# Joining two stages of a fused block: the mixer runs into the latent attention without a barrier, and three column sums move into the attention

## The chip, the cores and the metric

One core of a Trainium2 chip runs the whole program. The metric is the device time of one execution in microseconds, the median over several executions. The chip's engines are TensorE (PE in the profile, with its weight loads as PEld), VectorE (DVE), ScalarE (ACT), GpSimd (POOL) and SyncE (SP, which issues the DMAs). Each works through its own list in order and waits for others on semaphores.

## The reference, cut to what matters

Two transformer-like blocks of two layers each run over 512 tokens of width 1024. The change is in the second block, in each of its two layers. Such a layer splits its projection in four branches:

```
y_a = conformer_conv(...)   # 31-tap convolution, then layer_norm over 256 features, then silu
y_b = hgrn2_bidir(...)      # gated scan; o = rms_norm per head of 64 features, times silu(g)
y_c = short_gated_conv(...)
y_d = mla(...)              # q, k normed over 96 features per head, rope, softmax(q k^T / sqrt(96)) v
cat = rms_norm_2(concatenate([y_a, y_b, y_c, y_d]))   # in four groups of 256 features
x = x + cat @ w_out ; then attention over mem (256 rows), then a feed-forward part
```

Three of the norms matter here: the root mean square of `y_b` per head (two slots of 128 features, so two sums), and the variance of `y_a` after its mean is taken off (one sum over 256 features).

## The kernel before, in words

Everything lies transposed: features on the 128 partitions, the 512 tokens along the free axis. A tile of 128 x 512 float32 is called a slot (`S[:, n, :]`). PSUM has eight banks of 128 x 512. A norm is made of three steps: ScalarE squares the slots, TensorE multiplies a constant matrix (`ones` for a sum over all features, `heads` for sums over 64) with the squares, and ScalarE turns the sum into a factor by a logarithm and an exponential with scale -0.5. Both functions and the square stand in one table set.

The second block's layer is three stages, each a `nc.Block()` in which every engine gets its list: `second_mixer`, `second_attention` (called latent attention here) and `second_tail`. A stage closes with `sem.stage_end()` (line 334 on): all engines meet in a barrier, and the stage's semaphores, a contiguous range of numbers, are cleared by one instruction (line 337), so that the next stage can count them from zero.

**The end of the mixer.** After the scan, PE makes the projections of queries, keys and values, the mean of branch A (L1917), a rotation (L1921), `key_sum(0..3)` (L1904, the sum over 96 features for each head's key) and between them the query sums (L1931, 24 small products of 4 columns). Then come the products in question: two with `heads` for branch B into banks 5 and 6 (L1940) and two that add up the variance of branch A in bank 7 (L1943). ACT makes `key_root(h)` (a logarithm L2052 and an exponential L2054) for each head, in between the squares of branch B (L2066) and of the centred branch A (L2073), the copies of the values out of PSUM (L2069) and the query factor (L2076, L2078); it ends with three logarithms (L2083 twice, L2085). DVE makes `key(0)` (L2245), four `query_rope` (L2250), then `key(1..3)` (L2245), each of which needs its head's factor. POOL makes the rope part of the keys (L2311).

**The latent attention** has 16 units: four heads by four blocks of 128 queries. Unit n passes: PE scores (L743, a float32 product, which shows as two instructions of 128x512) into bank n mod 4; DVE maximum (L841) and its negative (L844); ACT exponential with its sum (L805); DVE reciprocal of the sum (L854), one step later; POOL scaling (L880) into a ring of four; PE transposes (L751) into bank 4 or 5, four units later; ACT copy to `PT` (L814); after eight units the product with the values (L757) into bank 6, and ACT's copy out (L823). PE goes in steps of two units, the others in steps of one. Bank 7 is used by nobody. Functions `side_act`, `side_dve`, `side_pool` and `side_pe` put other work behind each step. Before the change these are: a preamble of three exponentials on ACT (L2337), which finish the factors of which the mixer left the logarithms; from step 2 on ACT the squares of the memory input (L529), from step 3 on DVE its scaling (L523), its low part (L533) and the adding of squares (L540), eight of each; branch A times its factor on DVE in steps 3 and 4 (L2361), branch B in steps 5 and 6 (L2365); branch B times its gate on POOL at units 8 and 10 (L2380); weight tiles split in high and low parts on ACT (L367, steps 10, 12, 14) and POOL (L376, units 12 and 14). The input `mem` is loaded by SP at the stage's start (L2333). At its end ACT makes branch A's silu and the squares for the tail, and a barrier follows.

The order on each engine is written out by hand; nothing is planned at run time. A wait holds everything behind it on its engine.

Of the kernel before, what the change touches and what calls it, by code (L numbers as in the profile page):

```python
# [18 lines left out]
ALU = mybir.AluOpType  # L19
# [297 lines left out]
class Semaphores:  # L317


    def __init__(self, nc):  # L320
        self.nc, self.stream, self.stage, self.numbers = nc, {}, {}, []
        for name in ["tile_done", "tile_high", "tile_low"] + [f"tile_in_{i}" for i in range(RING)]:
            self.stream[name] = nc.alloc_semaphore(name)

    def __call__(self, name):
        if name in self.stream:
            return self.stream[name]
        if name not in self.stage:
            if len(self.stage) == len(self.numbers):
                self.numbers.append(self.nc.alloc_semaphore(f"stage_{len(self.numbers)}"))  # L330
            self.stage[name] = self.numbers[len(self.stage)]
        return self.stage[name]

    def stage_end(self):
        numbers = sorted(s.num for s in self.numbers)
        assert numbers == list(range(numbers[0], numbers[-1] + 1))
        self.nc.all_engine_barrier(sems_to_clear=range(numbers[0], numbers[-1] + 1))  # L337
        self.stage = {}

# [252 lines left out]
def build(nc, x_in, w1, small1, const_in, p_in, w2, small2, masks_in, mem_in, pos_in, out):  # L592
# [108 lines left out]

    def attention_work(*kinds, side_act=None, side_dve=None, side_pool=None, side_pe=None):

# [15 lines left out]
        def width(n):  # L719

            return units[n][0]["width"](units[n][3])
# [14 lines left out]
        def run_pe(pe):  # L736
            def scores(n):
                a, h, g, i = units[n]
                for m in range(a["maps"]):
                    s = first[n] + m  # L740
                    if s >= 4:
                        pe.wait_ge(sem("max_ready" if biased else "exp_done"), s - 3)
                    pe.matmul(banks[s % 4][:, 0:width(n)], a["q"](h, m, i), a["k"](h, m, width(n)), start=True,  # L743
                              stop=True).then_inc(sem("scored"), 1)

            def turn(n):
                pe.wait_ge(sem("prob_ready"), n + 1)
                if n >= 2:
                    pe.wait_ge(sem("pt_ready"), n - 1)
                for j in range(width(n) // P):  # L750
                    mm = pe.transpose(banks[4 + n % 2][:, j * P:j * P + P], prob(n)[:, j * P:j * P + P], cst("ident"))  # L751
                mm.then_inc(sem("transposed"), 1)
# [132 lines left out]

    def attention(weights, prefetch, work, before=None, first_act=None):

        run_pe, run_act, run_dve, run_pool = work
        with nc.Block() as block:
            @block.sync  # L890
            def _(sp):
                if before:
                    before(sp)
                weights.load(sp, prefetch)

            @block.tensor
            def _(pe):
                run_pe(pe)
# [8 lines left out]
            def _(dve):  # L907
                run_dve(dve)

            @block.gpsimd  # L910
            def _(pool):
                run_pool(pool)
        sem.stage_end()

# [786 lines left out]
    QUERY_R, EPS96 = 36, 54  # L1701
    B_R, DEVIATION, KEY_R = 36, 44, (45, 46, 47, 38)
    NL = len(LEVELS)
    PAD = 15

    def second_mixer(layer, weights, prep):

        base = DEPTH * FIRST_TILES + layer * SECOND_TILES
        latent_at = base + N_PROJ2
# [61 lines left out]
        with nc.Block() as block:  # L1771
# [6 lines left out]
            def _(pe):  # L1778
# [158 lines left out]
                pe.sem_inc(sem("tile_done"), 2)  # L1937
                for c in range(2):
                    pe.wait_ge(sem("b_square"), c + 1)
                    pe.matmul(banks[5 + c][:, :], cst("heads"), PT[:, 0, c, :], start=True, stop=True).then_inc(sem("b_sum"), 1)  # L1940
                for c in range(2):
                    pe.wait_ge(sem("centered_square"), c + 1)
                    mm = pe.matmul(banks[7][:, :], cst("ones"), PT[:, 0, 2 + c, :], start=(c == 0), stop=(c == 1))  # L1943
                mm.then_inc(sem("var_summed"), 1)

            @block.scalar
            def _(act):
# [115 lines left out]
                key_root(0)  # L2063
                for c in range(2):
                    act.wait_ge(sem("both"), c + 1)
                    act.activation(PT[:, 0, c, :], S[:, Y + 2 + c, :], ACT.Square).then_inc(sem("b_square"), 1)  # L2066
# [4 lines left out]
                for c in range(2):  # L2071
                    act.wait_ge(sem("centered"), c + 1)
                    act.activation(PT[:, 0, 2 + c, :], S[:, TAP_A + c, :], ACT.Square).then_inc(sem("centered_square"), 1)  # L2073
                act.wait_ge(sem("query_sum"), 1)
# [186 lines left out]
            def _(pool):  # L2261
# [50 lines left out]
        sem.stage_end()  # L2312

# [14 lines left out]
    def second_attention(layer, weights, memory):  # L2328

        base = weights.used  # L2330

        def before(sp):
            sp.dma_start(S[:, MEM_RAW:MEM_RAW + 4, :].rearrange("p a (b n) -> p (a b) n", b=2), mem_in).then_inc(sem("load_mem"), 16)  # L2333

        def first_act(act):
            for slot in (DEVIATION, B_R, B_R + 1):
                act.activation(S[:, slot, :], S[:, slot, :], ACT.Exp, scale=-0.5).then_inc(sem("late_rstd"), 1)  # L2337

        def side_act(act, step):
            if step == 2:  # L2340
                act.wait_ge(sem("load_mem"), 16)
            if 2 <= step < 2 + KC:
# [12 lines left out]

        def side_dve(dve, step, place):
            if place == "end" and step in (3, 4):
                a = S[:, TAP_A + step - 3, :]
                if step == 3:
                    dve.wait_ge(sem("late_rstd"), 3)  # L2360
                dve.tensor_tensor(a, a, S[:, DEVIATION, :], ALU.mult).then_inc(sem("standard"), 1)  # L2361
            if place == "end" and step in (5, 6):
                c = step - 5
                y = S[:, Y + 2 + c, :]
                dve.scalar_tensor_tensor(y, y, s2("onorm", c), S[:, B_R + c, :], ALU.mult, ALU.mult).then_inc(sem("b_normed"), 1)  # L2365
            if place == "scores" and step == 3:
# [8 lines left out]
        def side_pool(pool, n):  # L2375
            if n in (8, 10):
                c = (n - 8) // 2
                y = S[:, Y + 2 + c, :]
                pool.wait_ge(sem("b_normed"), c + 1)
                pool.tensor_tensor(y, y, S[:, G + c, :], ALU.mult).then_inc(sem("branch_b"), 1)  # L2380
            if n in (12, 14):
                weights.split_low(pool, base + n // 2 - 5)

# [4 lines left out]
            query_col=lambda h, i: col[:, QUERY_R + 4 * i + h:QUERY_R + 4 * i + h + 1]),  # L2388
            side_act=side_act, side_dve=side_dve, side_pool=side_pool), before, first_act)

# [387 lines left out]
```

## Time and profile before

| what | value |
|---|---|
| median of 3 runs | 3219.67 us (3214.8 to 3219.79) |
| the profiled execution | 3216.99 us, of which the span is 3215.2 us |
| mean granted TensorE clock | 0.984 of full speed |
| PE busy | 3066.1 us, 95% |
| latent attention, first layer | scores from 1903.24 us, next stage from 1953.36 us |
| latent attention, second layer | scores from 2674.20 us, next stage from 2724.61 us |

PE's share of 95% is a mean over stages with different limits: in the large dense products it is never idle, in the two latent attentions it waits often. A row of the timeline gives the start, how long the merged instructions took from the first start to the last end, the engine, the line, the operation, output <- input, the shape and the count; in square brackets the engine's idle time before it and what ended that. The granted clock is in parts of 2.4 GHz: 1.00 is 2.4 GHz and 0.5 is 1.2 GHz.

### The profile page before, as it was taken

Reading aid. Unit: us, or ns where it says so; the run is one execution under the profiler, and the core shown is the slowest. Engines: PE = TensorE matmul, PEld = TensorE weight load, DVE = VectorE, ACT = ScalarE, POOL = GpSimd, SP = SyncE. Lnnn points to the kernel's source line nnn. Section 1 sums busy time; section 2 is a strip of 40 time slices with the busy share of each in tenths; the row PEclk is TensorE's granted clock in tenths of the full one; section 3 lists DMA queues with packets and bytes.
Section 4 is the critical chain, followed back from the end, with each engine's and each line's share of the span. In section 5 each row is a group of like instructions: output and inputs, shape, how many; then the busy total and the mean of one; then the engine's idle time right before and its main releaser. Section 6 shows DMA issues by size and latency. Waiting matters only on the chain. (4 is left out here: it accounts for less than half of the span.)

```text
span 3215.2 us, 38320 instructions
## 1 busy us (share of the span) xinstructions
PE 3066.1 (95%) x14320; PEld 2394.0 (74%) x14320; DVE 1623.4 (50%) x2468; ACT 1327.0 (41%) x2194; POOL 1581.0 (49%) x862
## 2 busy tenths in 40 slices
PE   8989999999998999999999988899999988989999
PEld 6766788888766678888887756688888764768887
DVE  3863357732467434775348764433324955543321
ACT  4445433333443554333343475532323257442221
POOL 5634655554764455555565443344444534344443
PEclk9999999999999999999999989999999998999999
DMA  4211233333221123333323102233333211223333
GB/s 135 67 59 47 79 101 96 98 106 105 92 69 60 52 67 99 98 99 108 105 87 97 48 20 66 60 98 99 98 104 100 67 34 33 72 73 98 99 99 105
DMA packets 73736, 265.07 MB, mean 82 GB/s; under 512 B 8656, under 2 KB 9168, under 8 KB 73168
## 3 DMA queue, kind: packets, MB, share of 16 engines
q1 hardware_dynamic: 73552, 262.62, 26.6%
q8 instruction: 115, 1.88, 0.2%
q14 instruction: 69, 0.57, 0.1%
HBM read 260.49 MB, written 2.10 MB: 82 GB/s over the span
## 5 line engine op out<-in xcount | busy, mean ns | idle before, releaser
L376 POOL TENSOR_TENSOR low<-raw,high 128x1024 fp32r<-128x1024 f32 x482 | 1179.7, 2449 | 1148.8 <-ACT high L367 1115.5
L391 PE MATMUL bank<-slot_r,low 128*128 128x512 f32 (+1 forms) x3648 | 1423.8, 390 | 0.0
L392 PE MATMUL bank<-slot_r,high 128*128 128x512 f32 (+1 forms) x3648 | 1423.4, 390 | 0.0
L390 PE MATMUL bank<-slot_r,high 128*128 128x512 f32 (+1 forms) x3328 | 1323.8, 398 | 44.2 <-POOL low L376 15.0
L367 ACT ACTIVATE high<-raw 128x1024 fp32r<-128x1024 f32 x482 | 507.5, 1055 | 900.4 <-PE bank L392 826.7
L392 PEld LDWEIGHTS bank<-slot_r,high 128*128 128x128 f32 x3648 | 688.6, 189 | 147.2
L391 PEld LDWEIGHTS bank<-slot_r,low 128*128 128x128 f32 x3648 | 689.7, 189 | 144.5 <-issue 5.8
L390 PEld LDWEIGHTS bank<-slot_r,high 128*128 128x128 f32 x3328 | 629.0, 189 | 214.8 <-issue 50.3
L1624 DVE SCALAR_TENSOR_TENSOR tmp<-padded,small,tmp 128x512 f32<-128x512 f32 x176 | 209.7, 1249 | 0.0
L880 POOL TENSOR_SCALAR tmp<-tmp,stat 128x512 f32<-128x512 f32 (+3 forms) x128 | 79.9, 625 | 144.9 <-DVE stat L854 119.7
L2111 DVE SCALAR_TENSOR_TENSOR slots<-padded,small,slots 128x512 f32<-128x512 f32 x128 | 132.9, 1096 | 0.0
L1615 DVE TENSOR_TENSOR padded<-bank,rs 128x512 f32<-128x512 f32 x88 | 60.3, 686 | 138.9 <-PE bank L392 129.2
L2707 DVE TENSOR_TENSOR tmp<-bank,rs 128x512 f32<-128x512 f32 x44 | 30.4, 692 | 192.0 <-PE bank L392 186.8
L533 DVE SCALAR_TENSOR_TENSOR slot_r<-slots,small,slot_r 128x512 fp32r<-128x512 f32 (+1 forms) x80 | 93.5, 1168 | 44.0 <-ACT slot_r L520 43.7
L814 ACT ACTIVATE PT<-bank 128x256 f32<-128x256 f32 (+3 forms) x160 | 71.6, 453 | 104.8 <-PE bank L757 60.3
L743 PE MATMUL bank<-slots 64*128 64x256 f32 (+4 forms) x384 | 94.6, 501 | 18.2 <-PEq L337 15.4
L2619 ACT ACTIVATE tmp<-tmp 128x512 f32<-128x512 f32 x44 | 27.8, 632 | 203.0 <-DVE tmp L2707 203.0
L2717 DVE TENSOR_TENSOR tmp<-bank,rs 128x512 f32<-128x512 f32 x16 | 11.1, 691 | 193.1 <-PE bank L392 193.1
L751 PE MATMUL bank<-const,tmp 128*128 128x128 f32 x432 | 73.8, 294 | 36.3 <-ACT PT L814 27.6
L1367 DVE TENSOR_TENSOR slot_r<-tmp,slot_r 128x512 fp32r<-128x512 f32 x48 | 75.7, 1576 | 59.2 <-ACT slot_r L2612 59.2
L751 PEld LDWEIGHTS bank<-const,tmp 128*128 128x128 f32 x432 | 52.7, 148 | 68.2 <-issue 39.3
L390 PE MATMUL bank<-pt_r,high 128*128 128x512 f32 x256 | 101.1, 395 | 0.0
(316 smaller groups left out, 3134.4 us busy)
## 6 DMA issues: line engine op xcount, KB each, us to landing
raw<-w SPq DMA_DIRECT2D x482, 512.0 KB, 3.5
slots<-x_in SPq DMA_DIRECT2D x4, 512.0 KB, 6.5
slots<-mem_in SPq DMA_DIRECT2D x2, 1024.0 KB, 4.7
out<-slots SPq DMA_DIRECT2D x8, 256.0 KB, 4.6
const<-const_in SPq DMA_DIRECT2D x1, 1095.5 KB, 10.2
padded<-p_in SPq DMA_DIRECT2D x2, 512.0 KB, 5.1
tmp<-masks_in SPq DMA_DIRECT2D x1, 512.0 KB, 11.0
small<-small SPq DMA_DIRECT2D x2, 231.5 KB, 2.9
```

The source lines that it names most:

```text
L367: act.activation(self.high[:, t % PARTS, :], self.raw[:, t % RING, :], ACT.Copy).then_inc(self.sem("tile_high"), 1)
L376: pool.tensor_tensor(self.low[:, t % PARTS, :], self.raw[:, t % RING, :], self.high[:, t % PARTS, :].bitcast(F32), ALU.subtract).then_inc( ...
L390: pe.matmul(acc, lhs[0], rhs[1], start=first, stop=False)
L391: pe.matmul(acc, lhs[1], rhs[0], start=False, stop=False)
L392: return pe.matmul(acc, lhs[0], rhs[0], start=False, stop=last)
L533: dve.scalar_tensor_tensor(self.pairs[c][1], self.xs[c], self.gain[c], self.pairs[c][0].bitcast(F32), ALU.mult, ALU.subtract).then_inc(sel ...
L743: pe.matmul(banks[s % 4][:, 0:width(n)], a["q"](h, m, i), a["k"](h, m, width(n)), start=True, stop=True).then_inc(sem("scored"), 1)
L751: mm = pe.transpose(banks[4 + n % 2][:, j * P:j * P + P], prob(n)[:, j * P:j * P + P], cst("ident"))
L880: pool.tensor_scalar(prob(n), tmp[:, E + s % 4, 0:width(n)], st(3, s), 1.0, ALU.mult, ALU.mult).then_inc(sem("prob_ready"), 1)
L1367: dve.tensor_tensor(parts[g][1], tmp[:, 6 + g % 2, :], parts[g][0].bitcast(F32), ALU.subtract).then_inc(sem("hidden_low"), 1)
L1624: dve.scalar_tensor_tensor(o, padded_t[:, s % 4, 15 - tap:15 - tap + SEQ], s1("conv_w", (2 - tap) * 2 * FC + ch), o, ALU.mult, ALU.add).th ...
L2111: ins = dve.scalar_tensor_tensor(o, src, s2(w, 2 * j + c), o, ALU.mult, ALU.add)
```

## The change

The barrier between `second_mixer` and `second_attention` is gone. Semaphores are now named by a part ("mixer" or "latent") and a name, so both stages can count in one stretch, and the attention names the mixer's semaphores for which it must wait. The barrier behind the attention stays. The two `heads` products and the variance product leave the mixer's PE list and go into the attention's steps 2, 4 and 6 ("turns"), all through bank 7, one after the other; their logarithm and exponential become ACT's side work of steps 3, 5 and 7; the squares go to the end of ACT's mixer list, into slots of their own. Branch B's scaling on DVE moves to steps 6 and 7, branch A's to 8 and 9; POOL's gate products move to units 10 and 12, its weight splits to 11 and 13. ACT's preamble of three exponentials is dropped.

```diff
@@ class Semaphores
+    def of(self, part, name):
+        key = (part, name)
+        if key not in self.stage:
+            if len(self.stage) == len(self.numbers):
+                self.numbers.append(self.nc.alloc_semaphore(f"stage_{len(self.numbers)}"))
+            self.stage[key] = self.numbers[len(self.stage)]
+        return self.stage[key]
@@ second_mixer, tensor
-                for c in range(2):
-                    pe.wait_ge(sem("b_square"), c + 1)
-                    pe.matmul(banks[5 + c][:, :], cst("heads"), PT[:, 0, c, :], start=True, stop=True).then_inc(sem("b_sum"), 1)
-                for c in range(2):
-                    pe.wait_ge(sem("centered_square"), c + 1)
-                    mm = pe.matmul(banks[7][:, :], cst("ones"), PT[:, 0, 2 + c, :], start=(c == 0), stop=(c == 1))
-                mm.then_inc(sem("var_summed"), 1)
@@ second_mixer, scalar (squares and logarithms leave their old places)
-                    act.wait_ge(sem("b_sum"), c + 1)
-                    act.activation(S[:, B_R + c, :], banks[5 + c][:, :], ACT.Ln, scale=1.0 / 64, bias=eps).then_inc(sem("b_root"), 1)
-                act.wait_ge(sem("var_summed"), 1)
-                act.activation(S[:, DEVIATION, :], banks[7][:, :], ACT.Ln, scale=1.0 / 256, bias=eps).then_inc(sem("deviation"), 1)
+                    act.activation(S[:, B_SQ + c, :], S[:, Y + 2 + c, :], ACT.Square).then_inc(sem("b_square"), 1)
+                act.wait_ge(sem("centered"), 2)
+                for c in range(2):
+                    act.activation(S[:, A_SQ + c, :], S[:, TAP_A + c, :], ACT.Square).then_inc(sem("a_square"), 1)
@@ end of second_mixer
-        sem.stage_end()
@@ second_attention
         def before(sp):
+            sp.wait_ge(mixer("v_evac"), 2)
+        def scores_ready(pe, n):
+            if n == 0:
+                pe.wait_ge(mixer("query_done"), 4)
+                pe.wait_ge(mixer("key_done"), 2)
+                pe.wait_ge(mixer("key_rope"), 2)
+                pe.wait_ge(mixer("key_log"), 3)
+            if n == 1:
+                pe.wait_ge(mixer("query_log"), 1)
+            if n == 3:
+                pe.wait_ge(mixer("key_done"), 4)
+                pe.wait_ge(mixer("key_rope"), 4)
+        def side_pe(pe, step, place):
+            if place == "turns" and step in (2, 4):
+                c = step // 2 - 1
+                if c == 0:
+                    pe.wait_ge(mixer("centered"), 2)
+                else:
+                    pe.wait_ge(sem("b_log"), 1)
+                pe.wait_ge(mixer("b_square"), c + 1)
+                pe.matmul(banks[7][:, :], cst("heads"), S[:, B_SQ + c, :], start=True, stop=True).then_inc(sem("b_sum"), 1)
+            if place == "turns" and step == 6:
+                pe.wait_ge(sem("b_log"), 2)
+                pe.wait_ge(mixer("a_square"), 2)
+                for c in range(2):
+                    mm = pe.matmul(banks[7][:, :], cst("ones"), S[:, A_SQ + c, :], start=(c == 0), stop=(c == 1))
+                mm.then_inc(sem("var_summed"), 1)
         def first_act(act):
-            for slot in (DEVIATION, B_R, B_R + 1):
-                act.activation(S[:, slot, :], S[:, slot, :], ACT.Exp, scale=-0.5).then_inc(sem("late_rstd"), 1)
+            act.wait_ge(mixer("query_rstd"), 1)
+            act.wait_ge(mixer("cos_done"), 1)
         def side_act(act, step):
+            if step in (3, 5):
+                c = (step - 3) // 2
+                r = S[:, B_R + c, :]
+                act.wait_ge(sem("b_sum"), c + 1)
+                act.activation(r, banks[7][:, :], ACT.Ln, scale=1.0 / 64, bias=eps).then_inc(sem("b_log"), 1)
+                act.wait_ge(sem("b_log"), c + 1)
+                act.activation(r, r, ACT.Exp, scale=-0.5).then_inc(sem("b_rstd"), 1)
+            if step == 7:    # the same for the variance: Ln, Exp into DEVIATION
...
         def side_dve(dve, step, place):
-            if place == "end" and step in (3, 4):      # branch A; branch B in (5, 6)
+            if place == "end" and step in (6, 7):      # branch B; branch A in (8, 9)
...
-            if n in (8, 10):
+            if n in (10, 12):
...
-            if n in (12, 14):
+            if n in (11, 13):
```

## Rows read from the trace of the kernel before

**Rows 1.** The page, engines' busy time over the whole span.

```profile
PE 3066.1 (95%) x14320; PEld 2394.0 (74%) x14320; DVE 1623.4 (50%) x2468; ACT 1327.0 (41%) x2194; POOL 1581.0 (49%) x862
```

**Rows 2.** Timeline of the first layer's joint: start, us, engine, line, operation, count.

```profile
1897.73 1.95 PE L1940 MATMUL bank<-PT,const 128*128 128x512 f32 x4
...
1899.53 1.88 PE L1943 MATMUL bank<-PT,const 128*128 128x512 f32 x4
...
1901.44 0.69 ACT L2085 ACTIVATE slots<-bank,const 128x512 f32<-128x512 f32 x1 [0.72 <-PE bank L1943]
...
1903.21 1.67 ACT L2337 ACTIVATE slots<-slots 128x512 f32<-128x512 f32 x3 [1.08 <-PEq L337]
1903.24 7.08 PE L743 MATMUL bank<-slots 96*128 96x512 f32 x12 [1.83 <-PEq L337]
```

**Rows 3.** Timeline of the second layer's joint.

```profile
2664.32 1.06 ACT L2069 ACTIVATE slots<-bank 128x512 f32<-128x512 f32 x2
...
2665.28 3.19 PE L1904 MATMUL bank<-tmp,const 96*128 96x512 f32 x4
...
2666.52 1.13 ACT L2073 ACTIVATE PT<-slots 128x512 f32<-128x512 f32 x2
...
2668.53 1.54 DVE L2245 SCALAR_TENSOR_TENSOR slots<-bank,small,slots 64x512 f32<-64x512 f32 x2
...
2669.91 0.63 ACT L2054 ACTIVATE slots<-slots 128x512 f32<-128x512 f32 x1
...
2670.57 0.76 DVE L2245 SCALAR_TENSOR_TENSOR slots<-bank,small,slots 64x512 f32<-64x512 f32 x1 [0.49 <-ACT slots L2054]
...
2674.20 5.39 PE L743 MATMUL bank<-slots 96*128 96x512 f32 x12 [1.83 <-PEq L337]
```

**Rows 4.** Timeline of the second layer's attention, units 0 to 12.

```profile
2676.31 0.78 ACT L805 ACTIVATE tmp<-bank,stat,col 128x512 f32<-128x512 f32 x1 [0.46 <-DVE stat L844]
...
2679.04 0.34 DVE L523 TENSOR_SCALAR slot_r<-slots,small 128x256 fp32r<-128x256 f32 x1
...
2680.36 0.68 DVE L841 TENSOR_REDUCE stat<-bank 128x1 f32<-128x512 f32 x1
...
2681.32 0.78 ACT L805 ACTIVATE tmp<-bank,stat,col 128x512 f32<-128x512 f32 x1 [0.83 <-DVE stat L844]
...
2682.57 0.41 ACT L529 ACTIVATE slots<-slots 128x256 f32<-128x256 f32 x1
...
2682.86 0.68 DVE L841 TENSOR_REDUCE stat<-bank 128x1 f32<-128x512 f32 x1
...
2687.99 0.69 DVE L841 TENSOR_REDUCE stat<-bank 128x1 f32<-128x512 f32 x1
...
2689.89 0.69 DVE L841 TENSOR_REDUCE stat<-bank 128x1 f32<-128x512 f32 x1
...
2694.30 1.26 POOL L2380 TENSOR_TENSOR slots<-slots 128x512 f32<-128x512 f32 x1
...
2694.54 1.17 DVE L523 TENSOR_SCALAR slot_r<-slots,small 128x256 fp32r<-128x256 f32 x1
...
2697.39 0.78 ACT L805 ACTIVATE tmp<-bank,stat,col 128x512 f32<-128x512 f32 x1 [0.43 <-DVE stat L844]
...
2699.45 5.35 PE L757 MATMUL bank<-PT,slots 128*64 128x512 f32 x16
```

**Rows 5.** Timeline of the first layer's attention, unit 11 and the first value product.

```profile
1927.86 0.78 ACT L805 ACTIVATE tmp<-bank,stat,col 128x512 f32<-128x512 f32 x1 [0.44 <-DVE stat L844]
...
1929.92 3.65 PE L757 MATMUL bank<-PT,slots 128*64 128x512 f32 x16
```

**Rows 6.** Windows at each attention's start: busy us by engine, granted clock after POOL's column.

```profile
1903.00:1911.00 8.00, 7.76 (x20) 3.75 (x21) 5.18 (x15) 5.75 (x13) 2.37 (x3) 0.79 0.38 131
...
2674.00:2682.00 8.00, 7.80 (x24) 3.78 (x24) 6.41 (x20) 6.31 (x14) 2.75 (x3) 1.00 0.38 131
```

**Rows 7.** Line L337, the barrier's instructions: ns min/median/max.

```profile
L337 POOLq EVENT_SEMAPHORE_RANGE_CLEAR  x13: 113/283/437, 26.4 to 3214.6; - x13
```

More of the change, by code:

```diff
@@ L320, in __init__ @@
     def __init__(self, nc):
-        self.nc, self.stream, self.stage, self.numbers = nc, {}, {}, []
+        self.nc, self.stream, self.stage, self.numbers, self.part = nc, {}, {}, [], ""
         for name in ["tile_done", "tile_high", "tile_low"] + [f"tile_in_{i}" for i in range(RING)]:
@@ L337, in stage_end @@
         self.nc.all_engine_barrier(sems_to_clear=range(numbers[0], numbers[-1] + 1))
-        self.stage = {}
+        self.stage, self.part = {}, ""
 class Weights:
@@ L884, in attention_work, with attention @@
         return run_pe, run_act, run_dve, run_pool
-    def attention(weights, prefetch, work, before=None, first_act=None):
+    def attention(weights, prefetch, work, before=None, first_act=None, first_dve=None, first_pool=None, joined=False):
         run_pe, run_act, run_dve, run_pool = work
@@ L911, in _ @@
             def _(pool):
+                if first_pool:
+                    first_pool(pool)
                 run_pool(pool)
-        sem.stage_end()
+        if not joined:
+            sem.stage_end()
     weights = Weights(sem, raw, high, low, [w1[l, t] for l in range(DEPTH) for t in range(FIRST_TILES)]
@@ L1706, in second_mixer @@
     def second_mixer(layer, weights, prep):
+        sem.next_part("mixer")
         base = DEPTH * FIRST_TILES + layer * SECOND_TILES
@@ L2063, in _ @@
                 key_root(0)
-                for c in range(2):
-                    act.wait_ge(sem("both"), c + 1)
-                    act.activation(PT[:, 0, c, :], S[:, Y + 2 + c, :], ACT.Square).then_inc(sem("b_square"), 1)
+                act.wait_ge(sem("both"), 2)
                 act.wait_ge(sem("v_projected"), 1)
@@ L2339, in side_act, with turn_ready @@
-        def side_act(act, step):
+        def scores_ready(pe, n):
[9 more added lines that the diff above has]
+                pe.wait_ge(mixer("key_rope"), 4)
+        def turn_ready(pe, n):
+            if n == 0:
+                pe.wait_ge(mixer("key_log"), 4)
@@ new lines, in first_act, with first_dve, first_pool @@
+        def first_act(act):
+            act.wait_ge(mixer("query_rstd"), 1)
+            act.wait_ge(mixer("cos_done"), 1)
+        def first_dve(dve):
+            dve.wait_ge(mixer("pv_done"), 8)
+        def first_pool(pool):
+            pool.wait_ge(mixer("query_done"), 4)
+            pool.wait_ge(mixer("key_sum"), 4)
+            pool.wait_ge(mixer("key_rope"), 4)
+        def side_act(act, step):
+            if step in (3, 5):
[6 more added lines that the diff above has]
+            if step == 7:
+                r = S[:, DEVIATION, :]
+                act.wait_ge(sem("var_summed"), 1)
+                act.activation(r, banks[7][:, :], ACT.Ln, scale=1.0 / 256, bias=eps).then_inc(sem("a_log"), 1)
+                act.wait_ge(sem("a_log"), 1)
+                act.activation(r, r, ACT.Exp, scale=-0.5).then_inc(sem("a_rstd"), 1)
@@ L2340, in side_act @@
             if step == 2:
                 act.wait_ge(sem("load_mem"), 16)
+                act.wait_ge(mixer("branch_c"), 2)
             if 2 <= step < 2 + KC:
@@ L2356, in side_dve @@
         def side_dve(dve, step, place):
-            if place == "end" and step in (3, 4):
-                a = S[:, TAP_A + step - 3, :]
-                if step == 3:
-                    dve.wait_ge(sem("late_rstd"), 3)
+            if place == "end" and step in (6, 7):
+                c = step - 6
+                y = S[:, Y + 2 + c, :]
+                dve.wait_ge(sem("b_rstd"), c + 1)
+                dve.wait_ge(mixer("b_square"), 2)
+                dve.scalar_tensor_tensor(y, y, s2("onorm", c), S[:, B_R + c, :], ALU.mult, ALU.mult).then_inc(sem("b_normed"), 1)
+            if place == "end" and step in (8, 9):
+                a = S[:, TAP_A + step - 8, :]
+                if step == 8:
+                    dve.wait_ge(sem("a_rstd"), 1)
+                    dve.wait_ge(mixer("a_square"), 2)
                 dve.tensor_tensor(a, a, S[:, DEVIATION, :], ALU.mult).then_inc(sem("standard"), 1)
[L2362 to L2365, printed above, removed]
             if place == "scores" and step == 3:
@@ L2388, in second_attention @@
             query_col=lambda h, i: col[:, QUERY_R + 4 * i + h:QUERY_R + 4 * i + h + 1]),
-            side_act=side_act, side_dve=side_dve, side_pool=side_pool), before, first_act)
+            side_act=side_act, side_dve=side_dve, side_pool=side_pool, side_pe=side_pe, scores_ready=scores_ready, turn_ready=turn_ready),
+            before, first_act, first_dve, first_pool, joined=False)
     def second_tail(layer, weights, memory, lead):
```

29 lines of the change are left out of this document (17 added, 12 removed).

## The prediction

> **What bounds the kernel now.** The page first: PE is busy 95% of 3215.2 us [rows 1], so at large the dense products set the time, and only stages in which PE waits can give anything. The two latent attentions are such stages, and both lie between barriers, so whatever comes earlier at the barrier behind them comes earlier at the end. The timeline of the joint shows what the change aims at: the sums of branch B and the variance hold PE from 1897.73 to 1901.41, ACT takes the last logarithm until 1902.13, the barrier lets go at 1903.2, PE has then been idle for 1.83 us, and ACT spends 1.67 us on three exponentials first [rows 2]. The second layer repeats it 771 us later: scores at 2674.20, first softmax exponential at 2676.31 [rows 3, 4]. Inside the attention the timeline of units 3 to 10 shows a DVE without idle time: a step lasts 2.50 us where it carries a piece of branch A or B (2680.36 to 2682.86) and 1.90 us where it does not (2687.99 to 2689.89) [rows 4]. From the value product on, PE and ACT set the pace, with hardly any side work left.
>
> **The start (per layer; clock times are those of the second layer).** PE's last product that stays in the mixer ends at 2665.28 + 3.19 = 2668.47 [rows 3]. Score 0 waits for key(1), the first of two instructions that start at 2668.53 and take 1.54 us, so about 2669.3 instead of 2674.20: PE is 4.9 us earlier. DVE is later than PE: key(3) follows at 2670.07 and takes 0.76, to 2670.8; the exponential can start 0.96 us after a maximum does (2680.36 to 2681.32, [rows 4]), so at 2671.8 as far as DVE is concerned. ACT is later still. The squares that stood between the key factors are gone from there (1.13 us each pair, [rows 3]), so the last key's logarithm can start when PE ends, at 2668.5; with its exponential (together 1.30 us, by the 0.69 and 0.63 of such a pair in [rows 2, 3], overlapping a little) it is through at 2669.8. Behind it stand the four squares, 2 x 1.13 = 2.26 us, to 2672.05. The first softmax exponential starts there instead of 2676.31: **gain 4.3 us**. The dropped preamble (1.67), the three logarithms, the barrier (1.08 on ACT) and the wait for the products are all inside that figure and are not counted again. The memory input's DMA now waits only for the value copies, which end at 2665.4 [rows 3] at the latest, far ahead of its first reader. The weight splits, two units earlier on POOL, issue their next load earlier; nothing waits for it before the barrier.
>
> **What is given back.** In steps 3, 5 and 7 ACT has a logarithm and an exponential more: 1.30 us. An ordinary ACT step (exponential, copy, square) is 1.66 us, from 2681.32 to the square's end at 2682.57 + 0.41 [rows 4]; with the pair it is 2.96. DVE asks for the memory square of that step in the next one, 1.1 us after its own step began (maximum 0.68, its negative and the scaling of 0.34 come first), and has 1.90 or 2.50 us per step. In step 3 there is no copy yet and the branch work has left DVE, so DVE is fast: I get the square at 2677.3 where DVE would take it at 2676.35, a stall of 1.0. In step 5 it is 2.96 against 1.90 with some slack in hand, 0.9; in step 7 0.2, since DVE's steps 6 and 7 now carry the branch work. **Loss 2.1 us.** DVE's own branch work (four pieces, about 0.67 us each by the difference of 2.57 and 1.90) moves from steps 3 to 6 to steps 6 to 9, all within DVE's busy stretch: nothing. PE's products through bank 7 (0.94 us per sum at full clock, 1.88 us for two in [rows 2]) lie in PE's idle time; each waits for the logarithm before it, and the scores behind are wanted over a microsecond later. If this cover goes, it costs what the second rival says.
>
> POOL's gate product at unit 8 ran beside DVE's step 10 and stretched the memory scaling there from 0.34 to 1.17 us [rows 4]. At units 10 and 12 the memory work is over: **gain 0.8**. The Trainium skill (GPSIMD Engine Reference, Specifications) says the two engines share their SBUF interfaces and contend when DVE uses two ports or two inputs. By that rule the weight split, moved to unit 11, would do no harm either, since DVE then reads maxima from PSUM; without the rule the sum would lose this 0.8.
>
> At step 10 ACT has its weight split of 1.06 us behind exponential and copy and is no longer waiting for DVE: about 0.4 of the lead is lost. So the exponential of unit 11, and with it the value product, come 4.3 - 2.1 + 0.8 - 0.4 = **2.6 us** earlier in the second layer. From there on the chain is ACT's and is unchanged.
>
> **The clock.** In the first layer the scores ran at a granted clock of 0.79 on the mean over 8 us, in the second at 1.00 [rows 6]; so unit 11 came 1927.86 - 1903.24 = 24.6 us after the first score there and 2697.39 - 2674.20 = 23.2 us here [rows 2 to 5], 1.4 us later. The value product was the other way round: 3.65 us at full clock in the first layer, 5.35 in the second [rows 5, 4]. In the new first layer: with full clock 2.6 + 1.4 = 4.0; at half clock each score takes 1.7 instead of 0.9 us and the new product stands between scores 3 and 4, so DVE waits for PE at unit 4, and I get 0.6. Half and half: 2.3. In the second layer: 2.6 at full clock, -0.8 at half; I take seven to three, 1.6. The value products may swap their clocks, 1.7 us each way per layer: zero in the mean, kept for the range.
>
> The Trainium skill (TensorE: Matmul & The Clock Gate, Part 1) says that an array that has been idle runs at half clock until it has been busy again. By that, taking out an idle 1.83 us speaks for the better case in both layers, 4.0 + 2.6 = 6.6. The trace does not decide it: the same 1.83 us was followed by half clock in one layer and not in the other.
>
> **The barrier's clear.** The joined stage has some 19 semaphores more than the mixer's 74. The clear took up to 437 ns [rows 7], about 6 ns for each; 0.1 us more in each of the four barriers that are left, 0.4 in all. Bounds: 0 if it hides, 0.5 if every one counts.
>
> **Sum:** 2.3 + 1.6 - 0.4 = 3.5 us, in [rows 1] terms 0.1% of the span. The profiled execution took 3216.99 us, 1.8 more than its span, and so would take 3213.5. The median shown is 2.7 higher than it, which gives 3216.2; since the other executions lie on both sides (3214.8, 3219.67, 3219.79), I put the median at 3215.5. A difference of less than 0.2%, 6.4 us, is about what a measurement of this kernel cannot tell from none.
>
> **The rivals.** *All of the joint comes through.* Full clock for scores and value products in both layers: 4.0 + 2.6, and 1.7 for the second layer's value product, is 8.3 less 0.4, so 7.9: 3219.67 - 7.9 = 3211.8. For it: the two layers before show each half of it. Against: every stretch of low PE activity in the trace is followed by half clock somewhere.
>
> *The sums are a serial chain.* Each of the three needs PE, ACT, and again PE before the next may use bank 7, and both engines wait in order, with scores, transposes and softmax exponentials queued behind. If nothing covers them, each costs its product (0.94 at full, 1.9 at half clock) and the pair (1.30): three make 6.7 to 9.6 us against a start gain of 4.3, so 2.4 to 5.3 lost per layer and 4.8 to 10.6 in all: 3224.5 to 3230.3, 3227 in the middle. It decides from the point at which a sum costs more than 4.3/3 = 1.4 us; I reckon 0.7 on the mean. Against it: ACT waited 0.83 us for DVE in unit 4 [rows 4]. For it: ACT's 2.96 us per step is above DVE's.
>
> *The clock falls where it stood.* 0.6 and -0.8, and 1.7 lost in the first layer's value product: 1.9 slower with the clear, 3221.6, which is no measurable change.
>
> *The start is not early.* If score 0 waits longer than I see (POOL's rope part of the keys, 1.26 us per head, is its other source), the gain shrinks to the barrier's 1.1 us per layer and is eaten by the chains: 3220 to 3222.
>
> **Chances.** My forecast 0.50, with its own range 3212 to 3219; all through 0.20; serial chain 0.12; clock 0.12; late start 0.06. The range 3210 to 3223 takes in all but the chain and the far edges. Faster by over 0.2% (below 3213.2) is most of the second case and a part of the first: 0.32. Slower by over 0.2% (above 3226.1) is the half of the chain and a little of the rest: 0.09. Within: 0.59.
>
> **What would show it.** Right: the first score about 5 us after the last key_sum's start, with no idle time of PE above 1 us before it; first exponential 4.3 us earlier relative to L1904; in steps 3 to 7 DVE waits for ACT's L529 by 2 us in sum and not for PE; the memory scaling stays at 0.34 us throughout; the value product 2.6 us earlier. Wrong: DVE idle before L841 for PE in step 4 or later; ACT idle before its new logarithms by over 0.5 us; the transposes late enough that ACT's copies wait for them before the first value product; or half clock in both stretches in both layers.

## The result and the profile after

The changed kernel takes 3223.3 us (median of 16 runs, 3220.42 to 3224.54) against 3215.64 us before (16 runs, 3210.57 to 3219.91): ratio 1.0023, 95% interval 1.0016 to 1.0029. It is 7.7 us slower where I had forecast 4 us faster. The forecast started from the 3219.67 us of three executions; over 16 the kernel before stands 4.0 us lower, so what is compared below is the change and not the absolute time. The profiled execution has a span of 3222.4 us. Its page, the engines' busy time, against [rows 1]:

```profile
PE 3067.1 (95%) x14320; PEld 2392.0 (74%) x14320; DVE 1625.2 (50%) x2468; ACT 1327.3 (41%) x2194; POOL 1582.8 (49%) x862
```

The busy times and counts are those of before within 2 us, so the loss is in waits and in slow products, not in work. The timeline of the first layer's joint, to be held against [rows 2], shows both:

```profile
1896.24 2.59 PE L1920 MATMUL bank<-tmp,const 96*128 96x512 f32 x4
...
1901.16 1.13 ACT L2089 ACTIVATE slots<-slots 128x512 f32<-128x512 f32 x2
...
1902.86 6.07 PE L750 MATMUL bank<-slots 96*128 96x512 f32 x8 [4.03 <-PEq L1787]
...
1906.07 0.78 ACT L814 ACTIVATE tmp<-bank,stat,col 128x512 f32<-128x512 f32 x1 [3.78 <-DVE stat L853]
```

PE's last key sum (L1920, L1904 before) ends at 1898.83, and then PE has nothing for 4.03 us, until something on its own queue at line L1787. That line is `with nc.Block() as block:` of the mixer. All that was taken out is the clearing barrier; the Block itself ends with a meeting of all engines. Its queue instructions in the first layer, with the ns that each took:

```profile
L1787 PEldq DRAIN  x1: 2673/2673/2673, 1896.2 to 1896.2; - x1
L1787 ACTq DRAIN  x1: 2729/2729/2729, 1899.6 to 1899.6; - x1
L1787 POOLq DRAIN  x1: 1554/1554/1554, 1900.3 to 1900.3; - x1
L1787 DVEq DRAIN  x1: 1525/1525/1525, 1900.3 to 1900.3; - x1
L1787 SPq EVENT_SEMAPHORE  x1: 17/17/17, 1902.5 to 1902.5; - x1
```

Each engine drains its list, ACT last (1899.6 + 2.73, the end of the four squares that the change had put there), and at 1902.5 all go on together. The kernel before has the same instructions at its line L1771, ahead of those of the clearing barrier (L337, [rows 7]); I had looked at the second and not at the first:

```profile
L1771 PEldq DRAIN  x2: 4713/4713/4713, 1896.7 to 2667.7; - x2
L1771 ACTq DRAIN  x2: 717/717/717, 1901.4 to 2672.4; - x2
```

The second thing is the rate of the scores. Eight instructions (four scores) take 6.07 us in the first layer and 6.91 in the second; before, twelve took 7.08 and 5.39 [rows 2, 3]. The windows of the first 8 us of each attention, to be held against [rows 6] (granted clock: seventh figure, behind POOL's):

```profile
1903.00:1911.00 8.00, 8.00 (x14) 3.42 (x15) 4.71 (x14) 3.66 (x10) 2.01 (x3) 0.71 0.36 131
2676.00:2684.00 8.00, 8.00 (x11) 3.39 (x12) 3.89 (x11) 3.01 (x8) 1.39 (x2) 0.59 0.38 132
```

0.71 and 0.59 instead of 0.79 and 1.00: half clock, 1.2 GHz, for about the first 4.8 and 6.5 us. Half clock did not begin in PE's idle time. In the second layer of the kernel before it is there during the last two key sums (first window), and it is back at full while the moved sums run (second window):

```profile
2665.30:2668.30 3.00, 3.00 (x7) 1.25 (x7) 2.91 (x4) 2.94 (x8) 1.26 (x1) 0.60 0.00 0
...
2669.30:2672.30 3.00, 3.00 (x8) 1.04 (x6) 1.50 (x2) 2.36 (x5) 2.50 (x2) 1.00 0.00 0
```

In the changed kernel the same key sums are slow too (first window), but behind them PE does nothing (second window, busy 0.00) and the clock stays at half until the scores:

```profile
2668.50:2671.90 3.40, 3.40 (x6) 0.96 (x5) 3.27 (x5) 2.01 (x5) 1.69 (x2) 0.55 0.00 0
2672.00:2675.90 3.90, 0.00 (x0) 0.00 (x0) 1.94 (x3) 3.38 (x6) 2.23 (x2) 0.50 0.00 0
```

So before the change the four products of the sums had stood in PE's 4 us, and by their end the clock was up again for the scores. The third thing is DVE's waits in the second layer's attention until the value product (us in total, times, longest):

```profile
DVE stat L850 <- PE bank L750: 6.1, 5, 4.0
DVE slots L545 <- ACT slots L534: 1.3, 2, 0.8
DVE stat L863 <- ACT tmp L814: 0.3, 1, 0.3
```

Before, in the same stretch of the second layer, it was one wait for the first score and nothing for the memory square:

```profile
DVE stat L841 <- PE bank L743: 4.0, 1, 4.0
DVE stat L854 <- ACT tmp L805: 0.2, 1, 0.2
```

For all kernels below I measure one stretch in the profiled execution, from the start of the product that sums the mean of branch A (L1917 before; up to there nothing was changed) to the first product of the tail. Before: 66.0 and 66.3 us in the two layers. Changed: 67.6 and 68.6, so 4.0 us more in the stretch, out of 7.2 us that the spans differ by. The first value product comes 42.9 and 44.8 us behind the same start, against 42.5 and 41.1 before: 0.4 and 3.7 us later, where the forecast had it 2.3 and 1.6 us earlier. Of the rest, 1.9 lies ahead of that product in the first layer (1889.35 against 1887.42) and most of the remainder in the last tail, where the code is the same; these parts I did not trace to a cause. A single execution is not the median: over the 13 kernels of this document the stretch of the first layer starts anywhere from 1882.6 to 1889.6 us, though the code ahead of it does the same work in all. Therefore the medians say what a kernel gains, and the traces where.

### The profile page after: what moved, and what is told of

Same layout as the page of the kernel before. It is cut to its first block and busy times, and to the rows that moved or that the text cites. A ratio compares the mean times of both kernels' runs of the same rounds, so it can differ in the third digit from the quotient of the medians.

```text
span 3222.4 us, 38332 instructions
## 1 busy us (share of the span) xinstructions
PE 3067.1 (95%) x14320; PEld 2392.0 (74%) x14320; DVE 1625.2 (50%) x2468; ACT 1327.3 (41%) x2194; POOL 1582.8 (49%) x862
## 6 DMA issues: line engine op xcount, KB each, us to landing
tmp<-masks_in SPq DMA_DIRECT2D x1, 512.0 KB, 10.9
```

## The experiments

Each has its time against the kernel before on the same chip (medians of that: 3215.46, 3215.31 and 3215.39 us in the three groups), and an interval for the ratio.

**How much is the meeting, and how much the move of the sums?** Four kernels fill a table of three by two: two meetings, the Block's only, or none; sums kept in the mixer or moved.

```diff
@@ one Block: both stages put their lists in one
+        with nc.Block() as block:
+            shared[0] = Shared(block)      # entering it again gives the same block
             second_mixer(layer, weights, lead)
+            sem.next_part("latent")
             memory = memory_prep()
             second_attention(layer, weights, memory)
+        shared[0] = None
+        sem.stage_end()
```

> The changed kernel with mixer and latent attention in one Block, so that no engine meets another between them. Theory M (the meeting at the Block's end stayed, and the sums left PE with nothing to do ahead of it): the first score starts about 4 us earlier relative to key_sum's last product, right behind key(1), and no DRAIN stands between; per layer 3 to 4.5 us less than the changed kernel, 3215 to 3218 us where that takes 3223.3. Theory S (the sums are a serial chain that costs by itself): the score starts early, but the first value product does not come more than 1 us earlier; 3221 to 3223.

> Only the clearing barrier between mixer and attention is taken out (names by part, waits on the mixer's semaphores); the three sums, their squares and logarithms, ACT's three exponentials and the steps of the side work stay where they were before the change. Theory M: the meeting at the Block's end stays, so only the second meeting goes: 0.9 us per layer, less 0.5 for the longer clears: 1 to 2 us faster than before (3215.6 becomes 3214). Theory S: the same; if the whole joint were worth its 4 us without the sums' move, 3208.

> As the one before, and both stages in one Block: no meeting at all, sums kept in the mixer. Theory M: PE goes from the variance product to score 0 with under 0.5 us between instead of 1.8, so 1.5 to 2.5 us per layer faster than before, 3211 to 3213. Theory S says the same here and that this is the best of the four; theory M says that the kernel with one Block and moved sums is about as fast.

> The sums moved as in the change, and the clearing barrier put back between the stages (both meetings as before the change). This prices the move alone. Theory M: 0.9 us per layer slower than the changed kernel and 0.5 us back from shorter clears: 3224 to 3226, about 9 us slower than before; PE idle about 5 us ahead of score 0, which then runs at half clock. Theory S: the same total, but with the loss in steps 3 to 9 of the attention and not in its first four scores.

| median us, ratio to before (95%), stretch by layer | sums kept | sums moved |
|---|---|---|
| both meetings | 3215.5 (before), 66.0 / 66.3 | 3222.6, 1.0019 (1.0010 to 1.0027), 68.2 / 67.7 |
| the Block's only | 3216.8, 1.0002 (0.9993 to 1.0011), 64.2 / 64.2 | 3223.3 (changed), 1.0023, 67.6 / 68.6 |
| none (one Block) | 3211.5, 0.9989 (0.9980 to 0.9997), 63.2 / 63.2 | 3215.3, 1.0000 (0.9991 to 1.0008), 64.9 / 65.2 |

Down the columns: taking out the clearing barrier by itself gives nothing that can be measured (1.3 us slower and 0.7 slower, within the intervals), though the stretch with sums kept is 2 us shorter per layer in the trace; only the Block's end gives something, 8 us with sums moved, and 5.3 with sums kept, where the two intervals just overlap. Across: the move costs 7.2, 6.5 and 3.9 us; the first two are clear of the intervals, the third is not, and rests on the stretches, which are 1.7 and 2.0 us longer. So it is the move that makes the change slower, and the missing join that keeps it from being paid. The first and the third expectation came in (3215.3 and 3211.5 us). The second stood at 3214 and measured 3216.8, which is not told apart from it. The fourth missed: I had expected two meetings to be slower than one by another 1 to 2 us.

With one Block and sums moved, the second layer's joint is what I had drawn in the prediction:

```profile
2659.45 3.54 PE L1932 MATMUL bank<-tmp,const 96*128 96x512 f32 x4
2663.48 6.87 PE L750 MATMUL bank<-slots 96*128 96x512 f32 x8 [0.50 <-DVE slots L2261]
...
2666.69 0.78 ACT L814 ACTIVATE tmp<-bank,stat,col 128x512 f32<-128x512 f32 x1 [0.24 <-DVE stat L853]
```

Score 0 waits for key(1) and nothing else, 10.9 us behind the mean's product instead of 15.8: 4.9 us earlier, as forecast. The first softmax exponential comes at 14.1 instead of 17.9, 3.8 us earlier (forecast 4.3), since the scores run at 1.7 us each. The first value product comes 41.3 behind it in the second layer, against 41.1 before: nothing of the lead is left. (In the first layer it is 40.2 against 42.5, so 2.3 us are left there.) DVE's waits in the second layer from there to the value product:

```profile
DVE stat L850 <- PE bank L750: 2.5, 5, 0.7
DVE slots L545 <- ACT slots L534: 1.3, 2, 0.8
```

**Is it the clock?** The changed kernel, with products that nobody reads in PE's idle time.

```diff
                 pe.sem_inc(sem("tile_done"), 2)
+                pe.wait_ge(sem("centered"), 2)
+                for _ in range(4):
+                    pe.matmul(banks[7][:, :], cst("ones")[0:96, :], tmp[0:96, K_SQ + 3, :], start=True, stop=True)
```

> The changed kernel with four idle products (the shape of key_sum, into bank 7, read by nobody) at the end of the mixer's PE list, where PE has 4.0 us without work until the Block's end. Nothing of the order behind them changes. Theory C (the moved sums had kept PE's clock up; without them the first scores run at half clock): the scores go at full clock, the first softmax exponential comes 1 us and the first value product 2 to 3 us earlier relative to the mean's product, 4 to 6 us in all: 3218 to 3220. Theory S (the loss of the move sits in the logarithm and exponential steps of the attention): no more than 1 us, 3222 to 3224.

Measured 3216.1 us, ratio 1.0002 (0.9993 to 1.0011) against 1.0023 for the changed kernel: 7 us for work that does nothing, 2 us more than the clock theory had asked for. In the second layer PE stands idle for 0.56 us instead of 4.03, and eight score instructions take 3.67 us instead of 6.91:

```profile
2672.21 3.77 PE L1956 MATMUL bank<-tmp,const 96*128 96x512 f32 x8
2676.54 3.67 PE L750 MATMUL bank<-slots 96*128 96x512 f32 x8 [0.56 <-PEq L1787]
```

```profile
1904.00:1912.00 8.00, 7.86 (x25) 4.00 (x26) 5.56 (x17) 5.26 (x13) 2.30 (x3) 1.00 0.38 131
2676.50:2684.50 8.00, 7.96 (x25) 4.11 (x26) 5.66 (x17) 5.37 (x13) 2.31 (x3) 1.00 0.38 132
```

Full clock in both. Score 0 is later than in the changed kernel (14.6 us behind the mean's product against 13.5 and 14.4), and the stretch is still 1.3 and 1.9 us shorter. The first exponential comes at 16.8 in both layers (16.7 and 17.6 in the changed kernel), the value product at 42.6 and 41.6 (42.9 and 44.8): the expected 1 and 2 to 3 us are there in the second layer and hardly in the first. These 3.2 us of the stretch are about the difference of the two profiled executions (spans 3219.1 and 3222.4); the medians differ by twice that. The profiled execution of this kernel was the slowest of its 11, and where the other half of the median's gain lies no profile shows. The Trainium skill (TensorE: Matmul & The Clock Gate, Part 1) has the array at half clock after it was idle. The changed kernel alone does not show that, since its clock was at half already ahead of the 4.03 us; the kernel with early squares below does, in its first layer.

> One Block, sums moved, and one idle product between key_sum(3) and score 0, where PE waits 0.5 us for key(1). [...] If the clock does not rise sooner: 1 us slower per layer, 3217.

The same with one product between key_sum(3) and score 0, where one Block leaves PE 0.50 us without work in the second layer and 2.00 in the first: 3211.7 us, ratio 0.9988 (0.9979 to 0.9997), 3.6 us faster than one Block alone (the two intervals overlap), and not the 3217 of a clock that does not rise sooner. The windows of the first 8 us of the scores, for one Block alone and then with the product:

```profile
1894.00:1902.00 8.00, 8.00 (x14) 3.48 (x15) 6.13 (x16) 5.42 (x14) 3.47 (x5) 0.72 0.00 0
2663.50:2671.50 8.00, 8.00 (x12) 3.37 (x13) 5.34 (x13) 5.96 (x14) 3.16 (x4) 0.60 0.00 0
```

```profile
1900.20:1908.20 8.00, 8.00 (x15) 3.51 (x15) 6.35 (x16) 5.78 (x14) 3.70 (x5) 0.74 0.00 0
2669.60:2677.60 8.00, 8.00 (x25) 3.89 (x24) 6.58 (x18) 7.65 (x18) 3.84 (x5) 1.00 0.00 0
```

The clock rose sooner in the second layer and not in the first, in this one execution; the value product comes 40.0 and 38.9 us behind the mean's product, against 40.2 and 41.3.

**Is it the wait for the memory square?**

```diff
         def side_act(act, step):
+            if 2 < step < 2 + KC:
+                memory.square(act, step - 2)
             if step in (3, 5):
                 c = (step - 3) // 2
...
-            if 2 <= step < 2 + KC:
-                memory.square(act, step - 2)
+            if step == 2:
+                memory.square(act, 0)
```

> One Block, sums moved, and in ACT's side work of steps 3, 5 and 7 the square of the memory input stands ahead of the logarithm and exponential instead of behind. DVE waited for that square 0.50, 0.81 and 0.15 us. Theory S: these 1.5 us per layer come back, 3212 against 3215.3 for one Block alone. Theory C: under 1 us in all, since PE at half clock sets the early steps; 3214 to 3216.

3212.6 us, ratio 0.9986 (0.9978 to 0.9995): 2.7 us against one Block alone, nearly the 3 us of the waits. The value product comes 38.2 and 39.1 us behind the mean's product instead of 40.2 and 41.3, and DVE's wait for the square (1.3 us in the second layer) is gone from the trace. The medians' intervals overlap, so what carries this reading is the trace: the wait is the second cost of the move, beside the clock. It was 1.5 us per layer by the waits, and 2.0 and 2.2 by the value product.

**Is it the squares at the end of ACT's list?**

```diff
                 act.wait_ge(sem("both"), 2)
+                for c in range(2):
+                    act.activation(S[:, B_SQ + c, :], S[:, Y + 2 + c, :], ACT.Square).then_inc(sem("b_square"), 1)
...
                 key_root(1)
+                act.wait_ge(sem("centered"), 2)
+                for c in range(2):
+                    act.activation(S[:, A_SQ + c, :], S[:, TAP_A + c, :], ACT.Square).then_inc(sem("a_square"), 1)
```

> The changed kernel (two Blocks), with the four squares back at their old places among the key factors instead of at the end of ACT's mixer list. Theory M: the meeting waits for ACT, whose list ends with 2.2 us of squares, so score 0 comes up to 2 us earlier, and PE's idle time ahead of it is 2 us instead of 4: 4 us or more in all, 3217 to 3219. Theory C alone (only the clock matters): the same if the shorter idle time keeps the clock, 3222 to 3223 if the scores stay at half clock.

3222.7 us, ratio 1.0021 (1.0012 to 1.0029): nothing. Theory M fell; of theory C the number came in. ACT is through 2.2 us earlier, but the meeting then waits for POOL's rope parts of the keys, which end at 1899.58. In the changed kernel POOL had been only 0.5 us ahead of ACT (1901.74 against 1902.29). Score 0 comes 14.1 us behind the mean's product in both layers, against 13.5 and 14.4, and PE is idle for 5.24 us in the first layer and 3.78 in the second, both times slow behind it:

```profile
1897.09 2.49 POOL L2315 TENSOR_TENSOR slots<-rs,slots 32x512 f32<-32x512 f32 x2 [1.43 <-ACT slots L2063]
...
1900.20 6.13 PE L750 MATMUL bank<-slots 96*128 96x512 f32 x8 [5.24 <-PEq L1787]
```

In this first layer the key sums ended at full clock, at 1894.95. The granted clock was still 1.00 over the next 3 us without work and fell in the 2 us behind those, with PE idle:

```profile
1895.00:1898.00 3.00, 0.00 (x0) 0.00 (x0) 2.72 (x3) 2.90 (x7) 1.57 (x2) 1.00 0.00 0
1898.00:1900.00 2.00, 0.00 (x0) 0.00 (x0) 0.76 (x1) 0.25 (x1) 1.59 (x2) 0.58 0.00 0
```

**Can the parts be mended together, and which is best?** The first puts early squares, two idle products and the memory square first into the changed kernel with its two Blocks.

> The changed kernel with two Blocks and three mends at once: squares early, two idle products in the mixer's gap, the memory square ahead of the pair. If the causes found (list end on ACT, idle PE, DVE's wait for the memory square) are the whole loss of the change, it lands at or below the kernel before: 3211 to 3215. If something else in the move costs, it stays above 3216.

3216.2 us, ratio 1.0000 (0.9991 to 1.0009). At the edge of what was left open: the loss against before is gone, no gain has come, and it is no better than the idle products alone (3216.1). Its two idle products still leave PE 1.83 us without work, and in its first layer the scores ran at half clock again (7.06 us for eight instructions). With a meeting between the stages the moved sums buy nothing that these medians show.

> One Block, sums kept in the mixer, and ACT's three exponentials not ahead of the first softmax exponential but one each behind steps 0, 1 and 2. Exponential 0 then waits for DVE and not for ACT: 0.5 us per layer, and steps 1 and 2 have ACT time to spare: 3210 to 3211 against 3211.5 with the preamble. If the order on ACT there is worth nothing: 3211.5.

```diff
         def side_act(act, step):
+            if step < 3:
+                slot = (DEVIATION, B_R, B_R + 1)[step]
+                act.activation(S[:, slot, :], S[:, slot, :], ACT.Exp, scale=-0.5).then_inc(sem("late_rstd"), 1)
```

3211.9 us, 0.9986 (0.9977 to 0.9995): the same as with the preamble. The half microsecond is not seen in the total; exponential 0 came 16.0 us behind the mean's product in the second layer instead of 16.4. In the first layer it came at 14.3, but there the clock had never fallen and the key sums themselves were fast.

> One Block, the squares at their old places, branch B's first sum behind key_sum(3) in bank 5 (it fills PE's 0.5 us), the second sum and the variance together behind score 3 in banks 6 and 7, two logarithms in step 3, one exponential each in steps 4, 5 and 6, the memory square first. Theory C and S both expect it better than one Block alone (3215.3): no chain through one bank, no idle PE ahead of score 0. Against one Block with the sums kept (3211.5): score 0 comes 2.5 us earlier, exponential 0 1 us earlier, and the sums then stand between scores 3 and 4; 3208 to 3211.

```diff
@@ mixer, tensor: behind key_sum(3)
+                pe.wait_ge(sem("b_square"), 1)
+                pe.matmul(banks[5][:, :], cst("heads"), S[:, B_SQ, :], start=True, stop=True).then_inc(sem("b_sum"), 1)
@@ attention, side_pe: step 2, turns
+                pe.matmul(banks[6][:, :], cst("heads"), S[:, B_SQ + 1, :], start=True, stop=True).then_inc(sem("b_sum"), 1)
...
+                for c in range(2):
+                    mm = pe.matmul(banks[7][:, :], cst("ones"), S[:, A_SQ + c, :], start=(c == 0), stop=(c == 1))
```

3208.5 us, ratio 0.9980 (0.9971 to 0.9989): the lowest median, 6.9 us below the kernel before and 14.8 below the changed one. Its interval overlaps those of the kernels with one Block and sums kept (0.9989 and 0.9986), so that it beats them is likely and not shown. The windows of the first 8 us of the scores, and the timeline of the second layer's joint:

```profile
1896.30:1904.30 8.00, 8.00 (x22) 3.63 (x21) 6.43 (x18) 6.36 (x15) 4.52 (x5) 1.00 0.00 0
2664.00:2672.00 8.00, 8.00 (x22) 3.62 (x21) 6.43 (x18) 6.36 (x15) 4.56 (x5) 1.00 0.00 0
```

```profile
2659.66 3.27 PE L1932 MATMUL bank<-tmp,const 96*128 96x512 f32 x4
2662.73 1.45 PE L1967 MATMUL bank<-slots,const 128*128 128x512 f32 x2
2664.01 3.60 PE L750 MATMUL bank<-slots 96*128 96x512 f32 x8
2667.45 1.02 PE L2380 MATMUL bank<-slots,const 128*128 128x512 f32 x2
2668.31 1.88 PE L2384 MATMUL bank<-slots,const 128*128 128x512 f32 x4
```

PE has no idle time at all from the key sums to unit 5, the granted clock over the first 8 us of the scores is 1.00 in both layers, and the value product comes 37.5 us behind the mean's product in both layers, 5.0 and 3.6 earlier than before.

## Why the prediction was wrong, step by step

**The start (gain 4.3).** This is the step that failed first. It took for granted that without the clearing barrier score 0 waits for key(1) alone. The Block's own end stands between; score 0 came 13.5 and 14.4 us behind the mean's product instead of the 10.9 drawn, and the first softmax exponential 1.2 and 0.4 us earlier than before, not 4.3. Where the meeting is really taken out, score 0 comes 4.9 us earlier, the figure of the prediction. The rival for a late start was right that the start would be late, but its 3220 to 3222 lie 0.3 to 2.3 us above the 3219.67 from which it was reckoned, against a measured 7.7. Its cause, POOL's rope parts, was only next in line behind ACT's squares. That the change does not do what it says stood in no rival, and belonged there.

**The given back (2.1).** Right in kind, 0.6 us too high: DVE waited for the memory square 0.50, 0.81 and 0.15 us with one Block, forecast 1.0, 0.9 and 0.2; moving the square ahead took 2.7 us off the median.

**PE's products "lie in PE's idle time".** This failed the other way round. In the attention they do; in the mixer they had been what filled PE's time. The clock is at half when the key sums end, in the kernel before as in the changed one. With the sums behind them it was back at full for score 0; without, PE had 4.03 us of idleness and the scores began at half clock. I had weighed the clock, as luck of half and half, from a low first layer and a full second one, and had drawn idle time as removed; that the move creates it was not seen, and half clock in both layers, a sign of being wrong in the prediction's own list, is what came. In the first 8 us of each attention the granted clock went from 0.79 and 1.00 to 0.71 and 0.59, and idle products in the gap brought 1.00 twice and took 7 us off the median. The rival with the clock where it stood priced this at 0.6 us gained and 0.8 lost, on top of an early start. (Its sum also leaves out the clears: 0.6 - 0.8 - 1.7 - 0.4 is 2.3 us slower, 3222.0, not 1.9 and 3221.6.)

**POOL's 0.8.** Right: the memory scaling stayed at 0.34 us in every step up to the last (1.17 once before, [rows 4]).

**The clears (0.4).** Right: the clear took 565 ns where it took 437 [rows 7], 0.13 in each of four.

**The serial chain (3227).** In the difference it is the closest number of all (7.3 us slower in the middle, measured 7.7), and that is luck, since it was not the mechanism: PE had the next sum's logarithm in time at steps 4 and 6, and the chain's price was the memory square, 1.5 us per layer, not the 6.7 to 9.6 at which the rival had priced it.

## What to carry to other kernels

Before costing a barrier that is taken out, list every instruction of every queue between the two stages by its line: here one of two meetings stayed, and the one removed was worth nothing by itself. Work that is moved off an engine leaves a hole: if that engine is PE, read the granted clock at the edge of the hole, ask what clock the next products get, and leave some product in the hole, a useful one if there is one. When side work is added to a step, put behind it what nobody waits for, and ahead of it what another engine asks for next.

## What I had not expected of the hardware

Four products that compute nothing (3.77 us of PE) made the changed kernel 7 us faster. In one Block, PE idle for only 0.50 us between the key sums and score 0, half clock lasted from the key sums through most of the first four scores (granted clock 0.60 over 8 us of scores that kept PE busy without a break); with one product in that gap, idle or useful, the eight score instructions of the same layer took 3.60 us instead of 6.87. In the first layer the idle product did not help (5.70 us against 5.93), the useful one of the last kernel did. The two are not alike otherwise: the clock had fallen later where it did not help (last four key-sum instructions 2.48 us) than where it did (3.54). What decides between the two is not settled by these runs.

The fall itself belongs to every kernel here. In 24 of the 26 joints (13 kernels, two layers each, one execution of each) the granted clock goes to half during the key sums that follow the 24 products of 4 columns; PE is busy all that time, and while the small products run the clock still shows 1.00. What comes behind them goes with how the scores begin:

| PE between the key sums and score 0 | joints | granted clock at score 0 |
|---|---|---|
| idle 0.50 to 4.56 us, clock at half when PE stopped | 9 | half in all 9, for the next 4 to 7 us |
| other products, then idle 0.56 to 1.83 us, clock back at full when PE stopped | 8 | full or nearly so in 7, half in 1; it fell again within the first scores in 2 of the 7 |
| no idle time | 8 | full in 7, half in 1 |
| idle 5.24 us, clock at full when PE stopped | 1 | half |

An idle time of 0.50 us was followed by half clock and one of 0.56 us by full clock, so its length alone does not tell them apart; the clock with which PE went into it does, in all but one of the first 17 joints of the table. That is what one execution of each kernel shows, and no run was made to separate the two. In these joints a product in the hole pays by letting the clock come back before the scores.
